# Sums of squares moved into the output projection, a shared residual, and the feed-forward norm applied after its matmuls

## What is computed

```python
def rmsnorm(x, g):
    y = x * lax.rsqrt(jnp.mean(x * x, axis=-1, keepdims=True) + RMS_EPS)
    return y * g

def finish_layer(x, m, g_post_mix, g_pre_ffn, g_post_ffn, w_gate_up, w_down):
    x = x + rmsnorm(m, g_post_mix)                       # norm 2 and the residual
    return x + rmsnorm(swiglu(rmsnorm(x, g_pre_ffn), w_gate_up, w_down), g_post_ffn)

def swiglu(h, w_gate_up, w_down):                        # h is norm 3 of x
    g, u = jnp.split(h @ w_gate_up, 2, axis=-1)
    return (jax.nn.silu(g) * u) @ w_down
```

## Time and profile before

| what | value |
|---|---|
| median of 3 runs | 2564.36 us (2563.03 to 2570.11) |
| profiled execution, device time | 2567.03 us |
| its span, first to last instruction | 2565.4 us |
| mean granted TensorE clock | 0.969 |
| busy: TensorE, its weight loads, DVE, ACT, POOL | 2372.6, 2153.3, 1024.8, 856.5, 417.3 us |

### The profile page before, as it was taken

One profiled execution on the slowest core, in us unless ns is written; L12 is line 12 of the kernel. 1 busy time (PEld: TensorE's weight loads), 2 busy tenths in 40 slices (PEclk: granted clock), 3 DMA queues, 4 the chain that ended last, 5 costly groups with the idle time before them and its releaser, 6 DMA issues.

```text
span 2565.4 us, 45356 instructions
## 1 busy us (share of the span) xinstructions
PE 2372.6 (92%) x18306; PEld 2153.3 (84%) x18306; DVE 1024.8 (40%) x1359; ACT 856.5 (33%) x985; POOL 417.3 (16%) x852
## 2 busy tenths in 40 slices
PE   7999999997899998998888986999999999899996
PEld 6999999996666666666588965999999999899995
DVE  6443434333333333333255344333333333344444
ACT  3223233232333324333222233433343343233322
POOL 2010000002333323333210000111111111122210
PEclk8999999998999999999999998999999999899998
DMA  8454344536999999999756433767676776688871
GB/s 248 152 160 153 118 127 154 182 100 202 325 324 350 370 318 306 348 368 339 275 187 209 150 112 106 252 219 246 228 242 231 243 236 220 200 262 274 288 264 47
DMA packets 338964, 585.73 MB, mean 228 GB/s; under 512 B 20431, under 2 KB 282899, under 8 KB 334831
## 3 DMA queue, kind: packets, MB, share of 16 engines
q0 software_dynamic: 70704, 309.02, 34.2%
q1 hardware_dynamic: 268128, 274.86, 33.9%
HBM read 564.06 MB, written 109.39 MB: 263 GB/s over the span
## 4 chain that ended last, share of the span: by engine, by line
PE 77%; DMA 10%; DVE 4%; issue 4%; ACT 3%; POOL 1%; POOLq 0%; SPq 0%; DVEq 0%; ACTq 0%
PE ps L762 14%; PE ps L763 14%; PE ps L764 14%; DMA kraw<-in_cache_fox_k 5%; PE ps L807 5%; PE ps L809 5%; PE ps L808 5%; PE ps L996 3%; PE ps L1001 2%; PE ps L1021 2%; PE ps L985 1%; PE ps L1081 1%; PE ps L986 1%; PE ps L987 1%; DMA kraw<-in_cache_win_k 1%
## 5 line engine op out<-in xcount | busy, mean ns | idle before, releaser
L1485 DVE TENSOR_TENSOR w_lo<-raw,w_hi 128x2048 fp32r<-128x2048 f32 (+2 forms) x250 | 524.2, 2097 | 970.2 <-ACT w_hi L1199 970.2
L1199 ACT ACTIVATE w_hi<-raw 128x2048 fp32r<-128x2048 f32 (+2 forms) x250 | 439.2, 1757 | 927.8 <-PE ps L764 640.8
L762 PE MATMUL ps<-act_hi,w_hi 128*128 128x320 f32 x1664 | 516.0, 310 | 29.4 <-DVE act_lo L1514 22.5
L763 PE MATMUL ps<-act_lo,w_hi 128*128 128x320 f32 x1664 | 515.6, 310 | 0.0
L764 PE MATMUL ps<-act_hi,w_lo 128*128 128x320 f32 x1664 | 515.5, 310 | 0.0
L762 PEld LDWEIGHTS ps<-act_hi,w_hi 128*128 128x128 f32 x1664 | 313.5, 188 | 30.1 <-issue 30.1
L807 PE MATMUL ps<-act_hi,w_hi 128*128 128x320 f32 x1024 | 323.2, 316 | 3.3 <-DVE v_stage L1607 3.3
L809 PE MATMUL ps<-act_hi,w_lo 128*128 128x320 f32 x1024 | 317.2, 310 | 0.0
L808 PE MATMUL ps<-act_lo,w_hi 128*128 128x320 f32 x1024 | 317.1, 310 | 0.0
L763 PEld LDWEIGHTS ps<-act_lo,w_hi 128*128 128x128 f32 x1664 | 313.6, 188 | 0.0
L764 PEld LDWEIGHTS ps<-act_hi,w_lo 128*128 128x128 f32 x1664 | 313.5, 188 | 0.0
(11 more groups left out here) (339 smaller groups left out, 3663.6 us busy)
## 6 DMA issues: line engine op xcount, KB each, us to landing
raw<-in_w_gate_up SPq DMA_DIRECT2D x88, 1024.0 KB, 6.5
kraw<-in_cache_fox_k POOLq DMA_DIRECT2D x128, 512.0 KB, 6.9
vraw<-in_cache_fox_v POOLq DMA_DIRECT2D x128, 512.0 KB, 7.2
raw<-in_w_in SPq DMA_DIRECT2D x60, 1024.0 KB, 7.8
raw<-in_w_gate SPq DMA_DIRECT2D x32, 1024.0 KB, 14.1
raw<-in_w_down SPq DMA_DIRECT2D x32, 1024.0 KB, 6.1
out_win_k_sample<-in_cache_win_k POOLq DMA_DIRECT2D x64, 510.0 KB, 5.9
out_win_v_sample<-in_cache_win_v POOLq DMA_DIRECT2D x64, 510.0 KB, 4.1
```

The source lines that it names most:

```text
L762: pe.matmul(ps[:, bk_, 0:T], w_hi[:, slot, k, :], xh[:, x_k, :], start=(k == k0), stop=False)
L763: pe.matmul(ps[:, bk_, 0:T], w_hi[:, slot, k, :], xl[:, x_k, :], start=False, stop=False)
L1199: act.activation(w_hi[:, slot, 0:kt, :], raw[:, pslot, 0:kt, P * slot:P * slot + P], ACT.Copy).then_inc(hi_done, 1)
L1485: dve.tensor_tensor(w_lo[:, slot, 0:kt, :], raw[:, pslot, 0:kt, P * half:P * half + P], w_hi[:, slot, 0:kt, :].bitcast(F32), ALU.subtract) ...
```

## The change

1. In the output projection ACT squares every bank straight out of PSUM as it is finished. POOL adds 14 of the 15 first squares up in `ssum`, and TensorE sums `ssum` and the last square over partitions with 2 matmuls. DVE's read-out of the bank now multiplies by the gain of norm 2 and waits for that square. A dummy square root ahead of the last square loads ACT's table.
2. In each quarter DVE multiplies four blocks by `rstd` in one instruction, DVE adds two blocks to the residual and POOL the other two. ACT makes `act_hi` from residual times gain of norm 3, without `rstd`; DVE makes `act_lo` in four instructions.
3. TensorE begins the first two feed-forward units by quarters, as soon as a quarter's `act_lo` is there, and between them sums the squares of the new residual: four matmuls of 32 output columns each, into four groups of partitions of one bank. A copy of that bank to `xsum` and one more matmul give the sum for each token.
4. The `rstd` of norm 3 is applied when a gate or up bank is read out: the gate bank times `rstd` goes into the sigmoid, and the gate bank times `rr = rstd*rstd` replaces the bare bank in the product with the up bank.

```diff
 # POOL
             pool.dma_start(xT[:], scratch["xT"].rearrange("k p t -> p k t")).then_inc(xT_ld, 16)
-            pool.wait_ge(nrm_done, 8)
+            for e in range(1, KT - 1):
+                pool.wait_ge(o_sq, e + 1)
+                wait_pos(pool, o_add, e - 1)
+                pool.tensor_tensor(ssum[:], ssum[:], osq[:, e % 2, :], ALU.add).then_inc(o_add, 1)
+            pool.wait_ge(xT_ld, 16)
+            for q in range(4):
+                pool.wait_ge(up_n, q + 1)
+                part = slice(4 * q + 2, 4 * q + 4)
+                pool.tensor_tensor(xT[:, part, :], xT[:, part, :], outT[:, part, :], ALU.add).then_inc(x1_p, 1)
+            pool.wait_ge(x1_d, 4)
+            pool.wait_ge(x1_p, 4)
             pool.dma_start(scratch["x1T"].rearrange("k p t -> p k t"), xT[:]).then_inc(x1_st, 16)
 # TensorE
-            with pe.Fori(0, KT // 4) as i:
-                for k in range(4):
-                    unit(i * 4 + (U_OUT + k), k, act_hi, act_lo, KT, k % 2)
-            sum_squares(1)
-            sum_squares(2)
-            pe.wait_ge(nrm_done, 12)
-            with pe.Fori(0, FB // 2) as i:
+            for e in range(KT):
+                wait_pos(pe, o_sq, e - 3)
+                unit(U_OUT + e, e % 4, act_hi, act_lo, KT, e % 2)
+            pe.wait_ge(acc_free, U_UP + 1)
+            pe.wait_ge(o_add, KT - 2)
+            pe.matmul(ps[:, 7, 0:T], ones[:], ssum[:], start=True, stop=False)
+            pe.wait_ge(o_sq, KT)
+            pe.matmul(ps[:, 7, 0:T], ones[:], osq[:, 1, :], start=False, stop=True).then_inc(ss_mm, 1)
...
+            for q in range(4):
+                pe.wait_ge(up_lo, q + 1)
+                for k in range(4 * q, 4 * q + 4):
+                    mm = up_step(0, k)
+                if q == 3:
+                    mm.then_inc(unit_done, 1)
+                pe.wait_ge(x1_sq, 4 * q + 4)
+                for j in range(4):
+                    mm = pe.matmul(ps[32 * j:32 * j + 32, 6, 0:T], ones[:, 0:32], xsq[:, j, :], start=(q == 0), stop=(q == 3), **mmx)
+                mm.then_inc(x1_q4, 1)
+                if 0 < q < 3:
+                    pe.wait_ge(lo_done, U_UP + 2)
+                    for k in range(4 * q - 4, 4 * q):
+                        up_step(1, k)
+            for k in range(8, 12):
+                up_step(1, k)
+            pe.wait_ge(x1_sum, 1)
+            pe.matmul(ps[:, 7, 0:T], ones[:], xsum[:], start=True, stop=True).then_inc(x1_mm, 1)
+            for k in range(12, KT):
+                mm = up_step(1, k)
+            mm.then_inc(unit_done, 1)
+            for k in range(2, 4):
+                unit(U_UP + k, k, act_hi, act_lo, KT, k % 2)
+            with pe.Fori(1, FB // 2) as i:
 # ACT
+            def out_square(e):
+                act.wait_ge(unit_done, U_OUT + e + 1)
+                if e >= 3:
+                    act.wait_ge(o_add, e - 2)
+                dst = ssum[:] if e == 0 else osq[:, e % 2, :]
+                act.activation(dst, ps[:, e % 4, 0:T], ACT.Square).then_inc(o_sq, 1)
+
+            for e in range(KT - 1):
+                step(U_OUT + e, e % 4, 32 * (e // 4) + loads(U_OUT))
+                out_square(e)
+            act.activation(stat[0:1, 15:16], ones[0:1, 0:1], ACT.Sqrt)
+            out_square(KT - 1)
             root(1)
-            squares(2, xT, 4)
+            step(U_OUT + KT - 1, 3, 32 * (KT // 4 - 1) + loads(U_OUT))
+            for q in range(4):
+                for k in range(4 * q, 4 * q + 4):
+                    if k % 4 == 0:
+                        act.wait_ge(x1_d, q + 1)
+                    elif k % 4 == 2:
+                        act.wait_ge(x1_p, q + 1)
+                    ins = act.activation(act_hi[:, k, :], xT[:, k, :], ACT.Copy, scale=cols[:, 32 + k:33 + k])
+                ins.then_inc(up_hi, 1)
+                for k in range(4 * q, 4 * q + 4):
+                    wait_pos(act, x1_q4, q)
+                    act.activation(xsq[:, k % 4, :], xT[:, k, :], ACT.Square).then_inc(x1_sq, 1)
+            act.wait_ge(x1_q4, 4)
+            act.activation(xsum[:], ps[:, 6, 0:T], ACT.Copy).then_inc(x1_sum, 1)
             root(2)
-            high_parts(4, act_hi)
-            act.wait_ge(x1_st, 16)
             with act.Fori(0, FB // 2) as i:
                 for k in range(4):
                     step(i * 4 + (U_UP + k), k, i * 32 + loads(U_UP))
                     if k < 2:
-                        act.activation(sig[:, k, :], ps[:, k, 0:T], ACT.Sigmoid).then_inc(sg_done, 1)
+                        act.wait_ge(gr_ok, i * 2 + (k + 1))
+                        act.activation(sig[:, k, :], gr[:, k, :], ACT.Sigmoid).then_inc(sg_done, 1)
 # DVE
+            for e in range(KT):
+                if e < KT - 1:
+                    step(U_OUT + e, e % 4)
...
+                dve.wait_ge(o_sq, e + 1)
+                dve.tensor_scalar(outT[:, e, :], ps[:, e % 4, 0:T], cols[:, 16 + e:17 + e], None, ALU.mult).then_inc(acc_free, 1)
+            rms(1, ss_mm, 1)
...
+            for q in range(4):
+                b4, b2 = slice(4 * q, 4 * q + 4), slice(4 * q, 4 * q + 2)
+                dve.tensor_tensor(outT[:, b4, :], outT[:, b4, :], rstd[:].unsqueeze(1).broadcast_to([P, 4, T]), ALU.mult).then_inc(up_n, 1)
+                dve.wait_ge(up_n, q + 1)
+                dve.tensor_tensor(xT[:, b2, :], xT[:, b2, :], outT[:, b2, :], ALU.add).then_inc(x1_d, 1)
+                if q == 1:
+                    split_lo(1, 0, U_UP + 1)
+                dve.wait_ge(x1_d, q + 1)
+                dve.wait_ge(x1_p, q + 1)
+                dve.wait_ge(up_hi, q + 1)
+                for k in range(4 * q, 4 * q + 4):
+                    ins = dve.scalar_tensor_tensor(out=act_lo[:, k, :], in0=xT[:, k, :], scalar=cols[:, 32 + k:33 + k],
+                                                   in1=act_hi[:, k, :].bitcast(F32), op0=ALU.mult, op1=ALU.subtract)
+                ins.then_inc(up_lo, 1)
+            rms(2, x1_mm, 1, 32 * DM)
+            dve.tensor_tensor(rr[:], rstd[:], rstd[:], ALU.mult).then_inc(rr_ok, 1)
+            dve.wait_ge(rr_ok, 1)
+            def up_trip(i):
                 for k in range(4):
+                    dve.wait_ge(unit_done, i * 4 + (U_UP + k + 1))
                     if k < 2:
+                        dve.tensor_tensor(gr[:, k, :], ps[:, k, 0:T], rstd[:], ALU.mult).then_inc(gr_ok, 1)
+                    split_lo(k % 2, 1 if k < 2 else 0, i * 4 + (U_UP + k + 2))
+                    if k < 2:
+                        link(dve.tensor_tensor(gs[:, k, :], ps[:, k, 0:T], rr[:], ALU.mult))
                         dve.wait_ge(sg_done, i * 2 + (k + 1))
-                        dve.tensor_tensor(gs[:, k, :], ps[:, k, 0:T], sig[:, k, :], ALU.mult).then_inc(acc_free, 1)
+                        dve.tensor_tensor(gs[:, k, :], gs[:, k, :], sig[:, k, :], ALU.mult).then_inc(acc_free, 1)
...
```

More of the change, by code:

```diff
@@ L1163, in _, with up_step @@
             pe.wait_ge(acc_free, U_OUT + 2)
-            with pe.Fori(0, KT // 4) as i:
-                for k in range(4):
-                    unit(i * 4 + (U_OUT + k), k, act_hi, act_lo, KT, k % 2)
-            sum_squares(1)
-            sum_squares(2)
-            pe.wait_ge(nrm_done, 12)
-            with pe.Fori(0, FB // 2) as i:
+            for e in range(KT):
[6 more added lines that the diff above has]
+            pe.matmul(ps[:, 7, 0:T], ones[:], osq[:, 1, :], start=False, stop=True).then_inc(ss_mm, 1)
+            def up_step(u, k):
+                acc = ps[:, u, 0:T]
+                pe.matmul(acc, w_hi[:, u, k, :], act_hi[:, k, :], start=(k == 0), stop=False, **mmx)
+                pe.matmul(acc, w_hi[:, u, k, :], act_lo[:, k, :], start=False, stop=False, **mmx)
+                return pe.matmul(acc, w_lo[:, u, k, :], act_hi[:, k, :], start=False, stop=(k == KT - 1), **mmx)
+            pe.wait_ge(lo_done, U_UP + 1)
+            for q in range(4):
[22 more added lines that the diff above has]
+            with pe.Fori(1, FB // 2) as i:
                 for k in range(4):
@@ L1178, in _ @@
                         unit(i * 4 + (U_DOWN + 16 * kq + k), k, xh, xl, KQ, k % 2)
[L1179 to L1181 removed]
+            sum_squares()
+            pe.wait_ge(nrm_done, 8)
             for n in range(12):
@@ L1225, in root @@
                 act.activation(rstd[:], rstd[:], ACT.Sqrt).then_inc(rms_a, 1)
-            def high_parts(n0, dst):
-                for q in range(4):
-                    act.wait_ge(nrm_ready, n0 + q + 1)
-                    act.activation(dst[:, 4 * q:4 * q + 4, :], ntmp[:, q % 2], ACT.Copy).then_inc(nrm_hi, 1)
             act.wait_ge(neg_row, 2)
@@ L1422, in _ @@
                 step(U_OUT - 4 + k, k, loads(U_OUT - 4), KO if k < 2 else KT)
-            with act.Fori(0, KT // 4) as i:
-                for k in range(4):
-                    step(i * 4 + (U_OUT + k), k, i * 32 + loads(U_OUT))
-            act.wait_ge(acc_free, U_UP + 2)
-            squares(1, outT)
-            root(1)
-            squares(2, xT, 4)
+            def out_square(e):
```

(37 more changed lines are left out.)

44 lines of the change are left out of this document (20 added, 24 removed).

## The result

The changed kernel takes 2539.05 us (median of 4 runs, 2533.18 to 2548.84) against 2565.20 us for the kernel before (median of 4, 2563.03 to 2570.11): a ratio of 0.9897, 95% interval 0.9878 to 0.9916. The forecast was 2538.0, its range 2530 to 2547. On another chip the ratio was 0.9901 (0.9884 to 0.9918).

What follows compares the result with a forecast made beforehand. TensorE, busy 92% of the span, was taken as the bound, leaving its idle time or work to gain. 28.3 gained less 2.1 in the loop is 26.2 us off: profiled 2540.8, median 2538, range 2530 to 2547.

Steps and rivals of the forecast that it cites:

- Norm 2: After the output projection: rstd first used 4.8 us after the last projection matmul, against 20.8 before; other squares and sums cost nothing.
- The quarters: Between norm 2 and the last act_lo: 6.6 us each, 1.8 extra in quarter 1, 28.2 in all against 39.3 before.
- the case priced at 1.4: Quarter 1, where w_lo of unit 1 and POOL's read collide: if POOL goes first, the quarter grows by 1.4 us.
- No gain from sharing: Residual add in a quarter: all on DVE (1.49 us) would also give 6.6, so POOL's share gains nothing.
- The estimate of 1.4: POOL's add of 640 elements, estimated from the skill's 4497 ns for 2048, against the 1.3 us taken.
- The tail: After the last act_lo: norm 3's rstd and read-out leave TensorE idle 6.2 us; unit 2 ends at 54.5 against 82.85.
- unit 2 starts 46.0: In the tail: unit 2 waits for the first gate read-out, until 46.0 us after the last projection matmul.
- I add 1.4 for a slow start: Unit 2 behind the new idle time: 1.4 us for a low clock, bounds 0 and 1.5.
- slow-clock rival: Clock stays low through the quarters: backlog of 1.4 us and about 4 in the tail, 2543.7 in all; chance 0.12.
- The loop: Feed-forward loop: longer gate read-out eats the slack of 0.7 us, costing 2.1 us over 21 trips.
- A bubble between 0 and 0.2 in each of 21 trips. I take 0.1: TensorE's wait for the first gate unit's read-out in each loop trip: 0.1 us taken, 2.1 us in all.
- The sum: Whole kernel: 28.3 us gained up to the third unit's end, less 2.1 in the loop, makes 26.2.

Runs made afterwards that it cites:

- part1_only: Kernel before with only the projection squares, POOL's additions, two sums and the early table load; read-out without gain: 2552.41 us, ratio 0.9948.
- peel_warm: Changed kernel with first feed-forward trip written out and reordered, residual in two DVE instructions, dummy matmuls before and between quarters: 2528.39 us.

## Why the prediction was right

The total is right within 1.1 us, and the mechanism of most steps with it. That the number is so close is partly luck: two terms were off in opposite directions, by 2.9 and 2.1 us.

- **Norm 2.** 4.8 predicted, 4.6 measured. Its price beside other work is nothing, as costed: the 14 POOL sums take 2.7 us each with 4.3 us idle before them. `part1_only` shows the 16.2 us by itself.
- **The quarters.** 28.2 predicted, 28.15 measured, the last `act_lo` at 32.7 against 33.0. Inside a quarter, POOL took the 1.3 that I gave it with 0.1 over, and was held up behind DVE's add as argued. ACT's pair of copies takes 1.01 and not 0.83 (I priced a copy with a scale from a tile by a square); `act_lo` began at 4.9 in the quarter instead of 4.6 for both. In quarter 1 POOL went first, the case priced at 1.4, and the extra was 0.9 over its neighbours rather than the 1.8 I took. By luck that made up for the other quarters, which took 6.8 and not 6.6.
- **No gain from sharing** held, and understated it. I compared POOL with one DVE instruction, which it ties with (28.15 against 27.9). I didn't price DVE's two halves, which win 2.1. The rule of the Trainium skill (SBUF — State Buffer, "Summary: rules for kernel authors"), by which two engines with such operands block each other fully, is borne out by the 3.65 of `w_lo` beside POOL's read and its 2.28 to 2.29 without POOL: it ended at 1524.17, 2.15 after POOL's add, nearly its whole 2.29. The estimate of 1.4 from its GPSIMD Engine Reference ("Elementwise — side-by-side cycle accounting") agrees with POOL's ends 1.40 to 1.43 after DVE's.
- **The tail** is the step that was mis-sized: "unit 2 starts 46.0", measured 47.4, and "I add 1.4 for a slow start", measured 2.8 (9.85 for unit 2 against 7.04). Third unit at 57.4 against 54.5. The idle time of 6.2 us was right to 0.1, with the waits and the order that made it (`w_lo` ahead of `gs`). What failed is one assumption, the clock: I let the last quarter's 12 matmuls run at full clock (1.76 us, measured 3.36 from 1539.67 to 1543.03), and took the 1.5 that the slow start after the old gap cost as an upper bound for the new one. Half clock lasted 3 us there, 5.6 in `part1_only` and 6 here, so one row at the low level was no bound. My slow-clock rival put the price in the quarters as well; `peel_warm` shows that it isn't there.
- **The loop.** "A bubble between 0 and 0.2 in each of 21 trips. I take 0.1": it was 0.01 at most (28.17 against 28.16). The chain was right, 6.61 from `gr`'s start to `gs`'s end, and so was the lead of 0.3: half of it is the 0.15 that TensorE takes to start again behind `gs`, the other half that the last matmul's record ends 0.15 after the next is due. The read-out ends 0.08 short of costing: of the bounds 0 to 0.2 the lower one holds.
- **The sum.** The stage gave 25.4, not 28.3, and the loop took nothing, not 2.1: 25.4 against 26.2. That the medians agree within 1.1 is this, and luck besides: the runs of one kernel spread by 5 to 16 us.

## What to carry to other kernels

When a dependent chain is shortened so that work starts early, ask at once what the early work will run into: here the first units came earlier and ended before an idle time of 6.2 us, which cost another 2.8 of half clock, and all that the early start brought was lost until the order of ACT and DVE behind it was rewritten (8.4 us). Before giving part of an elementwise job to a second engine, price the first engine doing it in the same two pieces. And compare a stage between two marks in the trace, not totals, when runs spread by more than the effect.
